# Later sums of squares at the three input norms of a decoder layer (GpSimd starts them when VectorE's low parts are done)

## The reference

```
x += 1/2 * post1(SwiGLU_1(pre1(x)))          SwiGLU(h) = (silu(h @ w1) * (h @ w3)) @ w2, hidden width 2816
x +=       postM(mixer(preM(x)))              mixer: one projection W_in of 3080 columns, then
                                              4 mLSTM heads, 16 S5 groups, a short convolution, then W_out
x += 1/2 * post2(SwiGLU_2(pre2(x)))
pre(x) = x * rsqrt(mean(x*x) + eps) * g       (RMS norm over the 1024 features of a token)
```

## Time and profile before

| | us |
|---|---|
| runs (device time) | 1251.27, 1254.62, 1259.69; median 1254.62 |
| the profiled execution, its own time | 1256.27 |
| its span in the trace | 1254.4 |
| TensorE busy (matmuls) | 1169.3 (93%) |
| VectorE busy | 537.6 (43%) |
| ScalarE busy | 338.7 (27%) |
| GpSimd busy | 161.9 (13%) |
| mean granted clock of TensorE | 0.934 |

### The profile page before, as it was taken

How to read it: one execution, slowest core, us unless ns; L and a number is a source line. 1 busy time by engine, 2 the same in 40 slices (tenths; PEclk the granted TensorE clock), 3 DMA queues, 4 the chain that set the end, 5 groups by cost and what they waited for, 6 DMA issues and landing times.

```text
span 1254.4 us, 21696 instructions
## 1 busy us (share of the span) xinstructions
PE 1169.3 (93%) x9019; PEld 1128.8 (90%) x9019; DVE 537.6 (43%) x796; ACT 338.7 (27%) x426; POOL 161.9 (13%) x255
## 2 busy tenths in 40 slices
PE   5899999999999789999977999879999999999994
PEld 4899999999999779989975679869999999999994
DVE  5444433432334657733733333464343333333345
ACT  5322123221323333122530001233321222212231
POOL 3000708500000035001212200030000000000000
PEclk9999999999999869998985678959999999999997
DMA  5222322232222202211510002202222322222221
GB/s 206 68 84 84 92 93 84 84 87 96 72 93 76 80 17 78 93 59 61 127 28 17 34 17 93 85 18 85 84 84 85 91 92 84 84 86 99 75 75 71
DMA packets 30475, 97.86 MB, mean 78 GB/s; under 512 B 5848, under 2 KB 6104, under 8 KB 30296
## 3 DMA queue, kind: packets, MB, share of 16 engines
q1 hardware_dynamic: 30424, 97.14, 24.8%
HBM read 92.43 MB, written 4.70 MB: 77 GB/s over the span
## 4 chain that ended last, share of the span: by engine, by line
PE 86%; DVE 8%; ACT 2%; DMA 2%; issue 1%; POOL 0%; DVEq 0%; SPq 0%; ACTq 0%; POOLq 0%
PE ps L1477 76%; DVE xl L803 2%; PE ps L1567 2%; DVE x L843 2%; PE ps L1765 1%; DMA raw<-wout 1%; DVE y L839 1%; PE ps L1772 1%; PE ps L1546 1%; DVE wl L687 1%; PE ps L1719 1%; PE ps L1758 1%; ACT wh L402 1%; PE ps L1745 0%; PE ps L1783 0%
## 5 line engine op out<-in xcount | busy, mean ns | idle before, releaser
L1477 PE MATMUL ps<-xh,wh 128*128 128x272 f32 x1936 | 414.0, 296 | 43.8 <-DVE xl L803 35.3
L687 DVE TENSOR_TENSOR wl<-raw,wh 128x1024 fp32r<-128x1024 f32 (+1 forms) x169 | 206.8, 1224 | 521.7 <-ACT wh L402 521.1
L1477 PE MATMUL ps<-xl,wh 128*128 128x272 f32 x1936 | 407.2, 292 | 0.0
L1477 PE MATMUL ps<-xh,wl 128*128 128x272 f32 x1936 | 406.5, 292 | 0.0
L1477 PEld LDWEIGHTS ps<-xh,wh 128*128 128x128 f32 x1936 | 310.4, 193 | 51.5 <-issue 26.8
L1477 PEld LDWEIGHTS ps<-xl,wh 128*128 128x128 f32 x1936 | 312.1, 193 | 0.0
L1477 PEld LDWEIGHTS ps<-xh,wl 128*128 128x128 f32 x1936 | 310.5, 193 | 0.0
L402 ACT CAST wh<-raw 128x1024 fp32r<-128x1024 f32 (+1 forms) x169 | 173.7, 1028 | 493.6 <-PE ps L1477 482.4
L1477 PE MATMUL ps<-hh,wh 128*128 128x272 f32 x704 | 146.3, 289 | 0.5 <-DVE hl L702 0.5
L1477 PE MATMUL ps<-hl,wh 128*128 128x272 f32 x704 | 145.2, 287 | 0.0
L1477 PE MATMUL ps<-hh,wl 128*128 128x272 f32 x704 | 145.1, 287 | 0.0
(11 more groups left out here) (359 smaller groups left out, 752.1 us busy)
## 6 DMA issues: line engine op xcount, KB each, us to landing
raw<-w SPq DMA_DIRECT2D x120, 512.0 KB, 3.5
raw<-win SPq DMA_DIRECT2D x25, 512.0 KB, 3.5
raw<-w SPq DMA_DIRECT2D x16, 384.0 KB, 3.1
raw<-wout SPq DMA_DIRECT2D x8, 512.0 KB, 3.8
x<-xT SPq DMA_DIRECT2D x4, 544.0 KB, 6.3
o_yT<-x SPq DMA_DIRECT2D x8, 272.0 KB, 2.0
cs<-cT SPq DMA_DIRECT2D x1, 2048.0 KB, 8.6
o_sC<-cs SPq DMA_DIRECT2D x4, 512.0 KB, 2.6
```

The lines of the kernel that those rows point to most:

```text
L687: V.tensor_tensor(wl[par][:, 0:cols], raw[par][:, 0:cols], wh[par][:, 0:cols].bitcast(F32), ALU.subtract).then_inc(split_done, 1)
L1477: last = mm(ps[:, bank + s, 0:HALF], w[par][:, kk * P:(kk + 1) * P], a[:, kk, s * HALF:(s + 1) * HALF], start=(kk == 0 and i == 0), stop=( ...
```

## The change

`sum_squares` gets the tile count and the number of low parts as arguments, and waits for all eight low parts `xl` of its norm before the first add. ScalarE makes all eight `xh` first, and then the eight Squares; in FFN1 the cast of unit 1 goes between the two (`between`), in the mixer and FFN2 nothing does. TensorE's sums stand behind unit 2 in place of ahead of it, and in the mixer the spread, which stood within unit 2, stands behind the sums. No instruction but the wait is added, and none is removed.

```diff
                     elif f == 0:
-                        inputs()
-                        split(u0 + 1, (u0 + 1) % 2, half(1))
+                        inputs(lambda: split(u0 + 1, (u0 + 1) % 2, half(1)))
...
-            def inputs(g, ready):
+            def inputs(g, ready, between=lambda: None):
 
                 for kk in range(KD):
                     ready(kk)
                     nc.scalar.activation(xh[:, kk], x[:, kk], ACT.Copy, scale=norm_g[:, g, kk:kk + 1]).then_inc(xh_ready, 1)
                     cnt["xs"] += 1
+                between()
+                for kk in range(KD):
                     square(x[:, kk], lambda: None)
...
-            def sum_squares():
-
-                n = sum_squares.tiles
+            def sum_squares(n, low):
+
+                pool.wait_ge(xl_ready, low)
                 pool.wait_ge(xsq_ready, n + 2)
                 G.tensor_tensor(acc[:], act_t[:, n % 2], act_t[:, (n + 1) % 2], ALU.add).then_inc(xsq_used, 2)
...
+            sum_squares(0, KD)
...
+            sum_squares(KD, 2 * KD)
...
+            sum_squares(2 * KD + 4 + MH, 4 * KD)
...
                     if p == 0:
                         up(u0, hb, 0, lambda kk: pe.wait_ge(xl_ready, e0 + kk + 1))
                         up(u0, hb, 1)
+                        up(u0, hb, 2)
                         input_sums(7)
-                        up(u0, hb, 2)
                         spread(R_IN, 6, 7, 0).then_inc(bc_done, 1)
...
                 if i == 2:
+                    unit(u % 2, 4, KD, xh, xl)
                     input_sums(7)
-                    unit(u % 2, 4, KD, xh, xl, lambda kk: spread(16, 6, 7, 0).then_inc(bc_done, 1) if kk == 3 else None)
+                    spread(16, 6, 7, 0).then_inc(bc_done, 1)
```

More of the change, by code:

```diff
@@ L540, in _ @@
             nothing = lambda: None
-            tail = ffn(0, 0, 0, 0, 0, [nothing, nothing], lambda: inputs(0, x_loaded))
+            tail = ffn(0, 0, 0, 0, 0, [nothing, nothing], lambda between: inputs(0, x_loaded, between))
             def mix_split(i):
@@ L1287, in sum_squares @@
                 G.memset(stat[:, 61:62], 0.0).then_inc(xacc_ready, 1)
-            sum_squares.tiles = 0
-            sum_squares()
+            sum_squares(0, KD)
             pool.wait_ge(prm_in, 48)
@@ L1376, in _ @@
             signal(f_ready)
-            sum_squares.tiles = KD
-            sum_squares()
+            sum_squares(KD, 2 * KD)
             pool.wait_ge(x_new, KD)
@@ L1460, in _ @@
                 signal(cdec_ready)
-            sum_squares.tiles = 2 * KD + 4 + MH
-            sum_squares()
+            sum_squares(2 * KD + 4 + MH, 4 * KD)
         @block.tensor
```

## The result

| | changed kernel | kernel before, same chip | ratio, 95% interval |
|---|---|---|---|
| first comparison, median us | 1268.48 | 1258.22 | 1.008, 1.0045 to 1.0114 |
| later comparison, median us | 1264.63 | 1260.86 | 1.0047, 1.0026 to 1.0068 |

The change costs 6 to 10 us, 0.5 to 0.8%. The profiled execution took 1268.98 us (span 1267.1) against 1256.27 (1254.4).

What follows compares the result with a forecast made beforehand. TensorE was taken as bound, waiting most for `xl` (24.4 us of real gaps). 1256.3 + 0 (order) + 5 (clock) = 1261, put at 1260 on the runs' median; range 1249 to 1268 us.

Steps and rivals of the forecast that it cites:

- the stream: Input streams of FFN1, mixer, FFN2: without adds VectorE keeps 2.02 us steps; 6.9, 5.7 and 5.7 us earlier.
- the chain behind the Squares: All three stages: Squares wait for adds, the third unit's cast behind them; mixer's third unit at 461.3, hole 3.8 us.
- the bare round trip: After the third unit: variance, root, reciprocal no longer hidden; scales' copy 3.13 us after the sums' start.
- The sum of the order: Three input stages, clock left out: FFN1 -1.5, mixer +2.7, FFN2 -1.2 us, together 0.
- The 18 us of faster stream: Stream gains of the three stages, 18.3 us all together, forecast to be given back whole.
- the clock: Holes before the third units and the mixer's fourth: half clock costs 1.6 us for three of four, +5.
- the cheaper row: Mixer's first unit before the change: ten k-steps take 9.7 us, 2.2 us lost to the slow clock.
- the range: Whole kernel: 1249 to 1268 us, leaving out the first rival and most of the two slower ones.
- The stream's gain kept: Rival, input stages: 18.3 us less, less 1.1 for each of three round trips; 1241.3 or 1240 us; chance 0.07.
- `wl` early or the clock steady: Rival, third units: clock does not fall, or `wl` slips between two adds (3.3 us less); 1251 to 1256; chance 0.17.
- The clock deciding with six falls: Rival, holes before third and fourth units, all stages: 6 x 2.6 = 15.6 us, time 1270 to 1272; chance 0.09.
- The change doing nothing to `xl`: Rival, VectorE's stream: the long `xl` of 1.86 us are not GpSimd's doing; 1280 us; chance 0.04.

Runs made afterwards that it cites:

- again: The changed kernel run again without an edit, against the kernel before: ratio 1.0047 (1.0026 to 1.0068).
- after_third: The changed kernel traced a third time, without an edit: mixer's input 68.58 us, heads 113.39 us.
- filled kernel: The changed kernel with throwaway matmuls before unit 2 in all three stages and before the mixer's unit 3, against the kernel before: ratio 0.9974.

## Why the prediction was right or wrong

**Right: the stream.** VectorE's steps of 2.02 us, `xl` at 0.77, stream gain 5.3 to 5.7 us a stage. GpSimd's first add came 16.93 us after the stream's begin for 16.9 forecast.

**Right: the chain behind the Squares.** Unit 2 was forecast for 28.8, 461.3 and 29.0 us after FFN2's stream begin; it came at 28.82, 461.56 and 28.99 (855.46 less 826.47); `again` and `after_third` have 28.69 and 28.55 in FFN1, and 28.98 and 28.99 after the stream's start in the mixer. `wl` took 2.38 us for the exclusion with the last add. The cast moved ahead of the Squares turns the result from +0.6% to -0.5%, which shows the chain.

**Right: the bare round trip.** The sum of the order was 0. By the trace: with the slow share of the units taken out (1.5 in FFN1, 2.3 + 2.2 in the mixer, 1.7 in FFN2; see below), the stages are -1.6, +2.8 and -1.4 us, forecast -1.5, +2.7 and -1.2. Three traces of each kernel give -2.0, +3.2 and -1.3 in the mean. "The 18 us of faster stream are given back whole" holds. In FFN1 two slips of the working made little of it: 10.92 with three k-steps of 1.37 and five of 0.75 is 18.8 and not 18.4, and four k-steps were slow, so unit 1 began at 19.4 and the hole before unit 2 was 3.2 us and not 4.3. (The lower end of the range, added up as described, is 1250 and not 1249.)

**Wrong in size: the clock.** This is the term that was mis-sized: "so I take 1.6 us, somewhat under the cheaper row, for three of the four: +5." All four holes cost: 1.5 (7.65 for 6.12 us), 2.3 (8.42 for 6.10), 2.2 (8.37 for 6.19, the same unit 3 before from 473.59 to the next group at 479.78) and 1.7 (7.80 for 6.12), together 7.7 us; in `again` and `after_third` the same four units take 7.9 and 8.7 us more than at full clock. The filled kernel shows it for three of them and, in the length of unit 3, for the fourth. Not all of it is the change's: the kernel before loses 1.5 us in that unit 3 in two of its three traces, so that some 7 us are left, with which the stages' 7.0 (mean of three traces each) agree. Two readings led to the 5. One hole was left out of four, without a row that speaks for it. And the floor of the bounds, "0 (the nearest shorter wait, 2.58 us, costs none)", was one trace's luck: the same wait cost in the second. The holes were longer than forecast too in mixer and FFN2, 5.4 us for 3.8 and 3.3 (4.3 to 4.7 in the other two traces), because with a denser stream the clock was back at the end of unit 0 (in the mixer the k-steps at 446.82 and 448.21 show 0.52 for a pair, 0.82 at 453.53), so unit 1 ended sooner and the wait for unit 2 grew. The rule cited from the Trainium skill ("TensorE: Matmul & The Clock Gate", section "HAM oscillation — how this bites in real kernels") fits in that all four holes cost, in all three traces; that a unit restarts at half clock isn't so in the first trace's FFN1, where unit 2 began at full clock and fell 1.2 us in. The sum by it, +6.4, was nearer than mine.

**Wrong: the range and what it stood on.** The input stages cost 7.5 us (7.0 in the mean of three traces each), and the three ratios of the change (1.008, 1.0047, and 1.0066 without its wait) have a mean of 1.0064, or 8 us. 5 us was forecast. That error is small against the range; the median of 1268.48 lies 8.5 us above the forecast and 0.5 above the range because 1254.62, the median of three runs on which it was put, was itself low: beside the changed kernel the same kernel had 1258.22. And the range held nothing for stretches outside the change, such as the heads' 111.9 to 119.2 us. The bounds came from the terms of the sum alone.

**The rivals.** The stream's gain kept: false as the change stands; 12 us of it come back with the cast moved. `wl` early or the clock steady: false. The clock deciding with six falls: four holes cost, at 1.3 to 2.7 each and 2.0 in the mean, not 2.6, and FFN's fourth units did not need counting: FFN1's started slow (0.79 for its first pair at 40.60) but was covered, its next wait shrinking from 2.58 to 1.05 us, and FFN2's was at full clock (0.49) behind the same wait of 0.94 us. The change doing nothing to `xl`: false.

## What to carry to other kernels

When a producer is moved behind another on an in-order engine, follow that engine's next instruction and not the moved one: here eight Squares held back one cast of 1 us, and with it 5.4 us of TensorE. Count each new stand of TensorE at its length and at the half clock behind it; here four stands of 3.2 to 5.8 us cost 7.7 us more. Do not read from one trace that a wait costs nothing: one of 2.6 us did and did not, in two traces of one kernel. And put a range around the ratio, with the spread of the parts that aren't changed, not around three runs' median.

## What the runs showed of the hardware

- Throwaway matmuls kept the clock where they followed full work at once: 32 of them behind unit 1 took 4.1 us at 1.00 and unit 2 ran at full clock; 32 behind sums, spread and two waits of 0.7 us took 6.96 us at 0.56, 24 behind a wait of 1.96 us took 4.76. In the kernel with the cast first and 15 more around the sums, 32 took 4.23 us; no run separates the 15 from that kernel's other order.
- The length of a wait alone doesn't decide whether the clock falls: behind 2.58, 2.56 and 2.57 us FFN1's unit 4 began at full, half and full clock in three traces of the kernel before; behind 0.94 us unit 3 of the changed kernel began at half clock in FFN1 (40.60) and at full in FFN2 (867.39).
- Ten matmuls with one column took 2.29 us after a hole of 4.7 us (clock 0.50), 1.28 after one of 2.3 and 1.17 behind a unit.
- A stretch of 414 matmuls with many short waits (the heads) took 111.9 to 119.2 us with the same code.
